# Projections by token halves, norms inside the stage, attention on row halves: a two-block transformer kernel in fp32

## The chip, the cores and the metric

One core of one Trainium2 chip. The metric is the device time of the kernel in microseconds, median of three runs.

## What is computed

Three residual layers on x of 1024 tokens by 1024 channels, then a last norm. All of it is fp32.

```python
# layer 0 (even): attention and Fourier mixing; ctx: 256 context tokens
h = modulate(x, norm_g[0], shift, scale)                  # rms norm
proj = h @ w_in                                           # Fourier, q, k, v, gate
s = einsum('bqhmd,bkhmd->bhmqk', q, k) * DH ** -0.5       # 4 heads, 2 maps m, DH = 64, 1280 keys
p = softmax(s); a = p[:, :, 0] - lam * p[:, :, 1]         # difference of the two maps
o = einsum('bhqk,bkhv->bqhv', a, v)
ao = rms_norm(o, subln_g) * (1 - lam_init)
x = x + gate * ((concat([fourier_mix(u), ao]) * silu(g)) @ w_out)
# layer 1 (odd): x + gate * ((bg * conv3(cg * xt) * silu(g)) @ w_out)
# layer 2: h = rms_norm(x); y = sigmoid(m_a) * y_rglru + sigmoid(m_b) * y_hgrn2; x = x + y @ w_out
#          x = x + square(relu(rms_norm(x) @ w_up)) @ w_down
return rms_norm(x, norm_final)
```

## The kernel before

**Layout.** Channels lie on partitions, tokens along the free axis: X is [128, 8, 1024], eight tiles of 128 channels. A product of fp32 precision is made of three fp32r products: the weights are split in a high part Whi (ScalarE copies Wraw, L420) and a low part Wlo (POOL subtracts, L383), the operand in Hh and Hl. A **unit** is 128 columns of a weight matrix: per half of 512 tokens and per channel tile k a triple Whi x Hh, Whi x Hl, Wlo x Hh of 512 columns (`products`, L1282 to L1284, and `half`, L1392 to L1394), 48 products in all, into one of two accumulators `acc(0)`, `acc(1)` of two PSUM banks. Weights, too, have two slots: SyncE loads a slot (512 KB) when POOL has split the unit before last in it, ScalarE splits when TensorE has finished the unit that used Whi of this slot. Semaphores count units (`lo_ready`, `acc_ready`, `acc_free`). Stages follow each other in the list PHASES: four, q, k, v, g (even input), eo (even output projection, 8 units), oi (odd input, 32), oo (8), rg, hg (input of layer 2, 32 and 40), ho (8), mlp (64: four times 8 up and 8 down).

**Projections.** `dense` (PE) runs eight units for eo, oo and ho. For each unit VectorE adds the result to its tile of X (L829, L831), ScalarE squares the tile (L445), and TensorE sums the squares over partitions by a product with a matrix of ones in plain fp32 (`norm_sum`, L1296; one fp32 product of 512 columns shows as two half products in the trace). The sum of unit k is put behind unit k + 1. After the last one ScalarE takes the root (L434), VectorE the reciprocal of 1024 columns (L803), and then tile by tile a scaling (L809), the high part on ScalarE (L439) and the low part on VectorE (L814) in Hh and Hl; the next stage's first unit waits for each tile (`h_tile`). Before each projection all engines meet (`rendezvous`), and y (the input of the projection) is split into Hh and Hl (`split_y`, L449, L820): Y has to be whole, as Hh and Hl are the operand of the stage that makes it.

**Attention.** 32 blocks of 128 queries: all eight token blocks of head 0, then head 1, and so on, in a loop of two blocks. POOL copies the queries into a zeroed tile (L403), so that for map m only its 64 rows are filled. For each map: three fp32 products of 128 rows give 1280 scores in 2.5 PSUM banks (L1538), VectorE takes the maximum (L1028), ScalarE the exp with its sum (L601). VectorE combines both maps (L1035 to L1039). The ten transposes of the weights (L1552), their copies (L607), the ten products with v (L1559) and the scaled copy of the output (L612) run one block behind. `tile_pair` writes this order out for PE and ACT. After the loop the norm of the outputs, their transposes and the product with the gate follow on their own (L1052 to L1066), and x is loaded again (L635), since attention uses its place.

**End.** The last norm ("n4") writes X; TensorE transposes X back to token rows (L1754), ScalarE copies each of 8 row blocks (L794), SyncE stores it (L375).

Queues: SyncE issues all weight loads in the order of the units and the stores; ScalarE's queue loads tables, masks and x.

## Time and profile before

| | us |
|---|---|
| runs (3) | 3238.88, 3241.10, 3241.49 |
| median | 3241.1 |
| profiled execution, its own time | 3242.23 |
| its span | 3240.4 |
| TensorE busy (14314 products) | 3026.3 |
| VectorE, ScalarE, POOL busy | 1234.8, 918.5, 538.8 |
| mean granted TensorE clock | 0.965 of full |

The profile shows one execution. PE is TensorE's products, PEld its weight loads, DVE VectorE, ACT ScalarE, POOL GpSimd, SP SyncE. A busy time is the union of the instructions' times. Products overlap in the pipeline, so the spacing of their starts tells their cost, not their length. PEclk is the granted TensorE clock as a share of 2.4 GHz; 0.5 is 1.2 GHz.

### The profile page before, as it was taken

To read this page: it belongs to the slowest core of one execution; us is meant where nothing else is said; L and a number is where in the kernel's file an instruction comes from. 1 tells how busy PE (TensorE), PEld (TensorE's weight loads), DVE (VectorE), ACT (ScalarE), POOL (GpSimd) and SP (SyncE) were. 2 spreads that over 40 slices of the span, in tenths; PEclk is the share of its full clock that TensorE was granted. 3 is DMA by queue.
4 is the path that set the end of the run, shared out by engine and by line. 5 is a ranking of instruction groups with operands and counts; after the bars stand their busy time and mean duration, and the time that the engine had idled before them with its cause. 6 is when DMAs were issued, how large, how long until landed. Compare 5 with 4: busy or idle time off the path is not lost.

```text
span 3240.4 us, 36419 instructions
## 1 busy us (share of the span) xinstructions
PE 3026.3 (93%) x14314; PEld 2427.0 (75%) x14314; DVE 1234.8 (38%) x1284; ACT 918.5 (28%) x1027; POOL 538.8 (17%) x285
## 2 busy tenths in 40 slices
PE   6999989996889999889998999999897999999996
PEld 4878766664668887667777888888775888888874
DVE  4476126664232222244444566565524212121112
ACT  4332225552122122144442222222222202121221
POOL 0111100001112222112221111111011222222220
PEclk8999999997989999989999999999898999999998
DMA  6111520001111111111111111111010111111111
GB/s 200 65 33 39 176 78 0 0 7 72 32 39 45 52 45 46 33 39 45 45 45 42 33 40 33 33 36 37 20 39 26 46 52 45 52 45 47 50 46 52
DMA packets 249035, 155.11 MB, mean 48 GB/s; under 512 B 5360, under 2 KB 245360, under 8 KB 248432
## 3 DMA queue, kind: packets, MB, share of 16 engines
q1 hardware_dynamic: 247360, 146.10, 15.2%
q10 hardware_dynamic: 1584, 7.70, 0.6%
q8 instruction: 69, 1.13, 0.1%
q14 instruction: 22, 0.18, 0.0%
HBM read 149.59 MB, written 4.19 MB: 47 GB/s over the span
## 4 chain that ended last, share of the span: by engine, by line
PE 51%; issue 39%; POOL 4%; DVE 3%; ACT 1%; DVEq 0%; DMA 0%; POOLq 0%; ACTq 0%
PE PS L1282 8%; PE PS L1284 8%; PE PS L1283 8%; PE PS L1392 5%; PE PS L1394 5%; PE PS L1393 5%; POOL Wlo L383 4%; PE PS L1538 4%; PE PS L1650 3%; PE PS L1559 2%; PE PS L1552 1%; PE PS L1296 1%; PE PS L1655 1%; PE PS L1684 0%; PE PS L1638 0%
## 5 line engine op out<-in xcount | busy, mean ns | idle before, releaser
L383 POOL TENSOR_TENSOR Wlo<-Wraw,Whi 128x1024 fp32r<-128x1024 f32 (+1 forms) x216 | 519.4, 2405 | 2366.4 <-ACT Whi L420 2365.9
L1282 PE MATMUL PS<-Hh,Whi 128*128 128x512 f32 x1792 | 720.4, 402 | 78.5 <-DVE Hl L814 56.3
L1283 PE MATMUL PS<-Hl,Whi 128*128 128x512 f32 x1792 | 706.7, 394 | 0.0
L1284 PE MATMUL PS<-Hh,Wlo 128*128 128x512 f32 x1792 | 706.3, 394 | 0.0
L1282 PEld LDWEIGHTS PS<-Hh,Whi 128*128 128x128 f32 x1792 | 341.1, 190 | 175.6 <-issue 68.6
L1392 PE MATMUL PS<-Hh,Whi 128*128 128x512 f32 x992 | 400.4, 404 | 14.2 <-ACTq L277 8.9
L1283 PEld LDWEIGHTS PS<-Hl,Whi 128*128 128x128 f32 x1792 | 342.5, 191 | 73.2 <-issue 4.3
L1284 PEld LDWEIGHTS PS<-Hh,Wlo 128*128 128x128 f32 x1792 | 342.1, 191 | 72.7
L1394 PE MATMUL PS<-Hh,Wlo 128*128 128x512 f32 x992 | 388.1, 391 | 0.0
L1393 PE MATMUL PS<-Hl,Whi 128*128 128x512 f32 x992 | 387.7, 391 | 0.0
L420 ACT ACTIVATE Whi<-Wraw 128x1024 fp32r<-128x1024 f32 (+1 forms) x216 | 223.8, 1037 | 373.3 <-PE PS L1284 350.5
L1392 PEld LDWEIGHTS PS<-Hh,Whi 128*128 128x128 f32 x992 | 187.3, 189 | 58.3 <-issue 13.5
L1394 PEld LDWEIGHTS PS<-Hh,Wlo 128*128 128x128 f32 x992 | 186.9, 188 | 40.5
L1393 PEld LDWEIGHTS PS<-Hl,Whi 128*128 128x128 f32 x992 | 187.4, 189 | 36.7 <-issue 1.0
L1282 PE MATMUL PS<-Uh,Whi 128*128 128x512 f32 x512 | 202.2, 395 | 0.6 <-DVE Ul L1258 0.3
L1284 PE MATMUL PS<-Uh,Wlo 128*128 128x512 f32 x512 | 199.3, 389 | 0.0
L1283 PE MATMUL PS<-Ul,Whi 128*128 128x512 f32 x512 | 199.2, 389 | 0.0
L1261 DVE TENSOR_TENSOR X<-X,PS 128x1024 f32<-128x1024 f32 x32 | 39.1, 1221 | 307.1 <-PE PS L1284 307.1
L1538 PE MATMUL PS<-kT,qs 128*128 (+1 forms) x384 | 150.0, 527 | 5.3 <-POOL qs L403 2.7
L1255 DVE TENSOR_TENSOR sq<-ut 128x1024 f32<-128x1024 f32 x32 | 39.2, 1225 | 246.0 <-ACT ut L777 246.0
L445 ACT ACTIVATE sq<-X 128x1024 f32 (+1 forms) x32 | 33.9, 1060 | 329.5 <-PE PS L1296 145.4
L1538 PEld LDWEIGHTS PS<-kT,qs 128*128 128x128 f32 x384 | 68.9, 193 | 68.1 <-issue 68.1
(286 smaller groups left out, 3419.9 us busy)
## 6 DMA issues: line engine op xcount, KB each, us to landing
Wraw<-in_w_in SPq DMA_DIRECT2D x64, 512.0 KB, 4.0
adaV<-in_ada_w SPq DMA_DIRECT2D x16, 1024.0 KB, 5.2
Wraw<-in_odd_w_in SPq DMA_DIRECT2D x32, 512.0 KB, 4.0
Wraw<-in_w_up SPq DMA_DIRECT2D x32, 512.0 KB, 4.0
Wraw<-in_w_down SPq DMA_DIRECT2D x32, 512.0 KB, 3.9
Wraw<-in_even_w_in SPq DMA_DIRECT2D x24, 512.0 KB, 3.8
adaW<-in_ada_w SPq DMA_DIRECT2D x8, 1024.0 KB, 8.8
X<-in_x SPq DMA_DIRECT2D x8, 512.0 KB, 8.0
```

Source lines behind the costliest of these rows:

```text
L383: pool.tensor_tensor(Wlo[:, slot, 0:tiles, :], Wraw[:, slot, 0:tiles, :], Whi[:, slot, 0:tiles, :].bitcast(F32), ALU.subtract).then_inc(lo ...
L420: act.activation(Whi[:, slot, 0:tiles, :], Wraw[:, slot, 0:tiles, :], COPY).then_inc(hi_ready, 1)
L1255: tt(sq2[:, k % 2, :], ut[:, k % 2, :], ut[:, k % 2, :], ALU.mult).then_inc(sem("usq_ready"), 1)
L1282: mm(out, Whi[:, slot, k, :], hi[:, k, c], start=(k == 0), stop=False)
L1283: mm(out, Whi[:, slot, k, :], lo[:, k, c], start=False, stop=False)
L1284: last = mm(out, Wlo[:, slot, k, :], hi[:, k, c], start=False, stop=(k == kt - 1))
L1392: mm(out, Whi[:, slot, k, :], Hh[:, k, c], start=(k == 0), stop=False)
L1393: mm(out, Whi[:, slot, k, :], Hl[:, k, c], start=False, stop=False)
L1394: last = mm(out, Wlo[:, slot, k, :], Hh[:, k, c], start=False, stop=(k == KT - 1))
L1538: ins = mm(PS[:, 1536 * m + c:1536 * m + c + w].rearrange("p (a n) -> p a n", a=1), qs[:, s, m, :], kT[:, bass.ds(h, 1), c:c + w], start=T ...
L1559: ins = mm(bank(7, P), probT[:, s, t, :], vT[:, t, bass.ds(hc, P)], start=(t == 0), stop=(t == 9))
L1650: ins = mm(bank(4 + lev % 2, 64, c * 64).rearrange("p (b l) -> p b l", l=L), z, right, start=True, stop=True)
```

## The change

1. **Projections by token halves.** eo, oo, ho and the last down projection have 14 units in place of 8: tiles 0 and 1 over all tokens, then tiles 2 to 7 for tokens 0 to 511, then the same for tokens 512 to 1023. The weights of tiles 2 to 7 are loaded and split twice. After unit 7 the first half of X is complete.
2. **Norms within the stage.** VectorE adds the squares of a half in `sacc`, TensorE sums once per half. Root, reciprocal, scaling and splitting of the first half lie in units 8 to 12, those of the second half in the opening of the next stage, whose first two units run their first halves first. ScalarE now splits the weights of unit n + 2 before it squares tile n.
3. **Two operand regions in turn.** Stages read Hh, Hl or Bh, Bl (in the place of Y and of the scratch tiles), so y is split while it is made (oi: each tile; ho: in the last head) and the meetings of all engines before and after the projections go. The first eo and ho units run in quarters (four or two channel tiles) between the last operations of attention and of the last head.
4. **Attention.** Order by token block with the four heads inside; the two maps' queries lie in rows 0 to 63 and 64 to 127 of one tile, and each map is a product on its 64 rows. SCALE goes into the queries. The transposed weights have 2.5 banks of their own and one copy, outputs are squared on POOL and summed on VectorE per block, and the norm and transposes of the outputs run per token half.
5. **Output by channel.** X is stored as it lies, [128, 8 x 1024], in 8 stores, each when its two half tiles are scaled; the reordering to tokens is on the host. The 64 transposes and 8 copies go.
6. Loops over units are written out. The loads of x after attention are SyncE's.

```diff
-PHASES = [("four", 4), ("q", 4), ("k", 4), ("v", 4), ("g", 8), ("eo", 8), ("oi", 32), ("oo", 8),
-          ("rg", 32), ("hg", 40), ("ho", 8), ("mlp", 64)]
+PHASES = [("four", 4), ("q", 4), ("k", 4), ("v", 4), ("g", 8), ("eo", 14), ("oi", 32), ("oo", 14),
+          ("rg", 32), ("hg", 40), ("ho", 14), ("mlp", 70)]
...
+    Bh = at("Bh", y0, [KT, N], F32R)
+    Bl = at("Bl", t0, [KT, N], F32R)
...
+        def projection(i, base, shift):
+
+            def square(n):
+                evacuated(act, 0, 2, base + n)
+                act.wait_ge(sem("sq_added"), 13 * i + (0 if n < 2 else max(n - 2, 1)))
...
+            for n in range(14):
+                split_next(0, 2, base + n + 1)
+                square(n)
+                if n == 7:
+                    root(0)
+                if 9 <= n < 13 and i < 3:
+                    high(0, 2 * (n - 9))
+                    high(0, 2 * (n - 9) + 1)
+            root(1)
+            if i < 3:
+                for k in range(KT):
+                    high(1, k)
...
+            for n in range(14):
+                if n == 8:
+                    invert(0)
+                residual(n)
+                if n:
+                    add_square(n)
+                if 9 <= n < 13:
+                    for k in (2 * (n - 9), 2 * (n - 9) + 1):
+                        scaled(0, k)
+                    for k in (2 * (n - 9), 2 * (n - 9) + 1):
+                        if i < 3:
+                            low(0, k)
+            invert(1)
+            scaled(1, 0)
             for k in range(KT):
+                if k + 1 < KT:
+                    scaled(1, k + 1)
+                if i < 3:
+                    low(1, k)
...
+        def square_sum(i, h):
+
+            pe.wait_ge(sem("sq_added"), 13 * i + 6 * h + 7)
+            mm(bank(4 + h), ones, sacc[:, h, :], start=True, stop=True).then_inc(sem("ss_psum"), 1)
+
+        def by_halves(i, base, rhs):
+
+            for n in range(2, 14):
+                u, h = base + n, 0 if n < 8 else 1
+                claim(u)
+                c = slice(h * 512, h * 512 + 512)
+                for k in range(KT):
+                    last = triple(u, k, acc(u % 2)[:, 0:512], rhs, c)
+                    if n == 8 and k == 3:
+                        square_sum(i, 0)
+                last.then_inc(acc_ready, 1)
+
+        def opening(i, u, rhs):
+
+            pe.wait_ge(sem("norm_lo"), 16 * i + 8)
+            half(u, 0, rhs, lambda: square_sum(i, 1))
+            half(u + 1, 0, rhs)
+            c = slice(512, 1024)
+            for k in range(KT):
+                pe.wait_ge(sem("norm_lo"), 16 * i + 9 + k)
+                last = triple(u, k, acc(u % 2)[:, c], rhs, c)
+                if k % 2:
+                    triple(u + 1, k // 2, acc((u + 1) % 2)[:, c], rhs, c)
...
+        def scores(b):
+
+            s, h = b % 2, b % HEADS
+            pe.wait_ge(sem("qs_ready"), b + 1)
+            if b:
+                pe.wait_ge(sem("exp_ready"), 2 * b)
+            for i, (k1, w1, k0, w0) in enumerate(((0, 256, 0, 512), (256, 512, 512, 512), (768, 512, 1024, 256))):
+                mm(PS[:, S1 + k1:S1 + k1 + w1], qs[64:128, s, :], kT[64:128, h, k1:k1 + w1], start=True, stop=True).then_inc(sem("s1_psum"), 1)
+                if i == 2:
+                    pe.wait_ge(sem("s1_psum"), 3 * b + 1)
+                mm(PS[:, S0 + k0:S0 + k0 + w0], qs[0:64, s, :], kT[0:64, h, k0:k0 + w0], start=True, stop=True).then_inc(sem("s0_psum"), 1)
...
+        for c in range(BLOCKS):
+            scores(c)
+            if c >= 2:
+                turn(c - 2)
+            if c >= 3:
+                output(c - 3)
...
+        for c in range(BLOCKS):
+            if c >= 4:
+                output_out(c - 4)
+            if c >= 3:
+                weights_out(c - 3)
+            exps(c)
...
+        for c in range(BLOCKS + 1):
+            if c < BLOCKS:
+                shifts(c)
+            if c >= 1:
+                combine(c - 1)
+            if c >= 6:
+                block_sum(c - 6)
...
+        level(last, 4)
+        quad(o0, (0, 1), (Bh, Bl), odd_wait)
+        level(last, 5)
+        quad(o0, (2, 3), (Bh, Bl), odd_wait)
+        level(last, 6)
+        keys_turn(last)
+        quad(o0 + 1, (0, 1), (Bh, Bl), odd_wait)
+        increments(last)
+        quad(o0 + 1, (2, 3), (Bh, Bl), odd_wait)
+        output_rows(last)
+        quad(o0, (4, 5), (Bh, Bl), odd_wait)
+        output_turn(last)
+        quad(o0, (6, 7), (Bh, Bl), odd_wait)
+        quad(o0 + 1, (4, 5, 6, 7), (Bh, Bl), odd_wait)
+        by_halves(2, o0, (Bh, Bl))
...
-    out = nc.dram_tensor("out", (1, N, D), F32, kind="ExternalOutput").ap()
+    out = nc.dram_tensor("out", (P, KT * N), F32, kind="ExternalOutput").ap()
```

In `quad` a quarter of a unit is run for the channel tiles `ks` and the given halves; `claim` waits for the unit's weights and accumulator; `triple` is the three products above.

## Rows read from the trace of the kernel before

**Rows 1.** The profile page, part 1 and costliest groups (busy, mean ns | idle before, releaser).

```profile
PE 3026.3 (93%) x14314; PEld 2427.0 (75%) x14314; DVE 1234.8 (38%) x1284; ACT 918.5 (28%) x1027; POOL 538.8 (17%) x285
...
L383 POOL TENSOR_TENSOR Wlo<-Wraw,Whi 128x1024 fp32r<-128x1024 f32 (+1 forms) x216 | 519.4, 2405 | 2366.4 <-ACT Whi L420 2365.9
...
L420 ACT ACTIVATE Whi<-Wraw 128x1024 fp32r<-128x1024 f32 (+1 forms) x216 | 223.8, 1037 | 373.3 <-PE PS L1284 350.5
```

**Rows 2.** Busy time of each engine by stretch; columns as in its first line.

```profile
core 0: us, PE busy (x) PEld busy (x) DVE busy (x) ACT busy (x) POOL busy (x), PEclk, DMA share, GB/s
484.00:730.00 246.00, 228.84 (x1195) 154.96 (x1196) 147.33 (x198) 131.53 (x225) 17.70 (x54) 1.00 0.01 2
876.00:912.00 36.00, 16.21 (x33) 8.07 (x32) 29.30 (x19) 13.69 (x12) 0.65 (x1) 0.61 0.00 0
912.00:1256.00 344.00, 344.00 (x1513) 284.52 (x1511) 69.71 (x47) 66.76 (x62) 76.65 (x32) 1.00 0.17 49
1256.00:1260.00 4.00, 0.17 (x1) 0.00 (x0) 2.44 (x3) 2.39 (x3) 0.00 (x0) 0.93 0.00 0
1708.00:1718.00 10.00, 1.10 (x4) 0.65 (x3) 7.10 (x5) 3.73 (x4) 0.00 (x0) 0.77 0.10 22
2322.00:2358.00 36.00, 19.14 (x98) 17.47 (x97) 19.32 (x28) 7.03 (x8) 0.00 (x0) 0.68 0.00 1
```

**Rows 3.** Timeline of POOL and VectorE in oi (start, us, engine, operation [idle before, releaser]).

```profile
930.94 2.39 POOL L383 TENSOR_TENSOR Wlo<-Wraw,Whi 128x1024 fp32r<-128x1024 f32 x1 [7.50 <-ACT Whi L420]
...
931.28 2.60 DVE L1084 TENSOR_SCALAR cv<-up,P 128x1024 f32<-128x1024 f32 x1 [0.25 <-issue]
...
974.46 2.39 POOL L383 TENSOR_TENSOR Wlo<-Wraw,Whi 128x1024 fp32r<-128x1024 f32 x1 [7.50 <-ACT Whi L420]
```

**Rows 4.** Timeline of one attention block.

```profile
573.31 2.31 PE L1538 MATMUL PS<-kT,qs 128*128 x6
...
573.98 1.55 DVE L1039 SCALAR_TENSOR_TENSOR prob<-prob,acol 128x1280 f32<-128x1280 f32 x1
...
575.66 1.49 DVE L1028 TENSOR_REDUCE acol<-PS 128x1 f32<-128x1280 f32 x1
...
575.67 1.09 PE L1552 MATMUL PS<-basic,prob 128*128 128x128 f32 x8
...
577.42 1.33 ACT L601 ACTIVATE prob<-PS,acol 128x1280 f32<-128x1280 f32 x1
...
579.74 2.49 PE L1559 MATMUL PS<-vT,probT 128*128 x20 [0.61 <-ACT probT L607]
```

**Rows 5.** Timeline of TensorE at attention's first and last products, and eo's first.

```profile
450.05 2.90 PE L1538 MATMUL PS<-kT,qs 128*128 128x512 f32 x3 [2.66 <-POOL qs L403]
...
724.75 2.31 PE L1538 MATMUL PS<-kT,qs 128*128 x6
...
734.96 4.63 PE L1559 MATMUL PS<-vT,probT 128*128 128x128 f32 x20 [0.47 <-ACT probT L607]
...
774.78 0.77 PE L1282 MATMUL PS<-Hh,Whi 128*128 128x512 f32 x1 [3.80 <-DVE Hl L820]
```

**Rows 6.** Timeline of eo: sums of squares, the reciprocal, the next stage's first product.

```profile
799.77 1.88 PE L1296 MATMUL PS<-sq,basic 128*128 128x512 f32 x4
...
875.65 1.88 PE L1296 MATMUL PS<-sq,basic 128*128 128x512 f32 x4
...
881.84 6.55 DVE L803 RECIPROCAL Rn<-Rn 128x1024 f32<-128x1024 f32 x1 [4.48 <-ACT Rn L434]
...
892.72 0.76 PE L1282 MATMUL PS<-Hh,Whi 128*128 128x512 f32 x1 [12.07 <-DVE Hl L814]
```

**Rows 7.** Groups of TensorE instructions by line.

```profile
L1296 PE MATMUL PS<-sq,basic 128*128 128x512 f32 x128 | 60.5, 595 | 4.0 <-ACT sq L445 4.0
```

**Rows 8.** DMA issues of the page (KB each, median us to landing).

```profile
Wraw<-in_w_in SPq DMA_DIRECT2D x64, 512.0 KB, 4.0
```

**Rows 9.** Timeline of the end: last sums of squares and the scaling.

```profile
3197.89 1.88 PE L1296 MATMUL PS<-sq,basic 128*128 128x512 f32 x4
...
3210.30 10.92 DVE L809 SCALAR_TENSOR_TENSOR X<-X,P,Rn 128x1024 f32<-128x1024 f32 x8
```

More of the change, by code:

```diff
@@ L1261, in dve_program, with claim @@
                 tt(X[:, k, :], X[:, k, :], acc(k % 2), ALU.add).then_inc(acc_free[k % 2], 1)
             dve.drain()
-        dve.drain()
-        norm("n4", X, N, None, None, lambda k: P2[:, COL2["norm_final_2"] + k:COL2["norm_final_2"] + k + 1], None)
+        projection(3, DOWN, plain, lambda k: P2[:, COL2["norm_final_2"] + k:COL2["norm_final_2"] + k + 1], None)
     def pe_program(pe):
         mm = pe.matmul
-        def products(i, n, b, rhs, start=0, kt=KT, first=False):
+        def claim(u):
+            pe.wait_ge(lo_ready, u + 3)
+            pe.wait_ge(acc_free[u % 2], u // 2 + 1)
@@ new lines, in triple, with half, whole @@
+            return mm(out, Wlo[:, u % 2, k, :], hi[:, k, c], start=False, stop=(k == KT - 1))
+        def half(u, h, rhs=(Hh, Hl), mid=None):
+            if h == 0:
+                claim(u)
+            c = slice(h * 512, h * 512 + 512)
+            for k in range(KT):
+                last = triple(u, k, acc(u % 2)[:, c], rhs, c)
+                if k == 3 and mid:
+                    mid()
+            return last
+        def whole(u, rhs):
+            half(u, 0, rhs)
+            half(u, 1, rhs).then_inc(acc_ready, 1)
@@ L1558, in output @@
             for t in range(10):
[L1559 removed]
+                ins = mm(PS[:, OUT:OUT + P], probT[:, b % 2, t, :], vT[:, t, h * P:(h + 1) * P], start=(t == 0), stop=(t == 9))
             ins.then_inc(sem("o_psum"), 1)
[L1562 to L1569 removed]
@@ new lines, in pe_program @@
+        turn(31)
+        output(30)
+        output_turn_half(0)
+        output(31)
+        quad(e0, A, (Hh, Hl), even_wait, (1,))
+        quad(e0 + 1, A, (Hh, Hl), even_wait, (0,))
+        output_turn_half(1)
+        quad(e0 + 1, A, (Hh, Hl), even_wait, (1,))
+        quad(e0, B, (Hh, Hl), even_wait)
+        quad(e0 + 1, B, (Hh, Hl), even_wait)
+        by_halves(0, e0, (Hh, Hl))
+        opening(0, BASE["oi"], (Bh, Bl))
+        for u in range(BASE["oi"] + 2, BASE["oo"]):
+            whole(u, (Bh, Bl))
@@ L1615, in pe_program @@
[L1615 removed]
+                claim(u)
                 if j == 4:
```

864 lines of the change are left out of this document (419 added, 445 removed).

## The prediction

> **What bounds the kernel now.** I read the page's totals first: TensorE is busy for 93% of the span [rows 1]. That average hides two kinds of stretch, so the table by stretch comes next. Inside a stage of plain products (912 to 1256) TensorE works for 344.00 of 344 us at full clock [rows 2]. Nothing there can be won. The time lies where it stops or does work that isn't a product of the model: the norm behind each projection (876 to 912: 16.21 us busy of 36), the hand-overs (1256 to 1260, 1708 to 1718, 2322 to 2358), the end, and attention, where it is 93% busy at full clock but with operands half full of zeros [rows 2]. The timelines of these places give the prices. About 0.2% (6.5 us) is what a measurement of this kernel can tell from no change.
>
> One unit of weights is 48 products of 512 columns. Four units of the odd input stage lie 974.46 - 930.94 = 43.52 us apart [rows 3], so a unit is 10.88 us and a half unit 5.44.
>
> **Attention loop.** Now a block of 128 queries pays two score sets of 2.31 us, ten transposes (8 in 1.09) and 20 half products in 2.49 [rows 4]: about 8.6 us. From the first score (450.05) to the end of the last (724.75 + 2.31) it is 277.0 us for 32 blocks [rows 4, 5].
> Afterwards the two maps sit on rows 0-63 and 64-127 of the array. If they run side by side, both sets take about what one takes, plus a lead-in: 2.4 us. TensorE's sum is then 2.4 + 1.3 + 2.5 = 6.2 us. The softmax loop is as long: scores 2.4; maximum of the last mixed bank 0.69 (estimate: 1280 elements take 1.49 [rows 4], so 0.16 + 1.04 ns each); a small maximum with its drain 0.3; exp 1.33; the second exp waits for a 1024-element maximum (1.22 by the same estimate) and starts at 5.2; it ends at 6.55, and the next scores wait for both. VectorE's sum (1.49 x 2, a second fixed part for each extra maximum, the combination 1.55 and its scalars) is about 6.3. Three engines within 0.4 us of each other don't mesh perfectly; I take 6.8 us a block. No row shows half-row products, so the bounds are 6.5 (side by side) and 8.5 (one after the other: 4.6 us of scores in the same loop). I take the side near 6.5, since two operands in disjoint rows share nothing the rows name. The zero fill and one copy go, so it starts 1 us earlier: last scores end at 449 + 31 x 6.8 + 2.4 = 662.2 against 727.1. **-64.9**.
>
> The Trainium skill ("TensorE: Matmul & The Clock Gate", Part 3) measured 3.07x for four row tiles, not 4x. Two tiles at that efficiency would take 3.0 us instead of 2.4 and the total would be about 3010. The same skill ("TensorEngine Tiling", Key Properties) says that a change of tiling mode drains the engine; each block changes twice. No row here shows either.
>
> **Attention's end.** Now from the last score to the first projection product (774.78) is 47.7 us, partly at half clock: the last output takes 4.63 us instead of 2.49 [rows 4, 5]. With 1.4 us lost to the slow first products this is 49.1. Afterwards squares and sums are made per block on POOL and VectorE, and four quarter units (10.9 us of projection) fill waits. Following ScalarE in order: two exps, table load and root, then copy, output, copy for blocks 28 to 31, the last output lands about 24 us after the last score; scale, turn, split of the second half some 10 us later. That is 34 us, less the 10.9 us of work done in it, plus 3 for a clock that won't stay up: 26. **-23**.
>
> **Three projections with their norm.** From 776.2 to the effective start of the next stage (its end 1256.2 less 32 units = 908.0) there are 131.8 us for 87.0 us of products: 44.8 us lost. It is: eight sums of squares, each 4 half products (units and sums alternate six times from 799.77 to 875.65, 75.88 / 6 = 12.65 us against 10.88, so 1.77 each, 14.1 [rows 6]; all 128 half products of the four norms: [rows 7]); and behind the last unit a root, a reciprocal of 6.55 us for 1024 columns, and the first split, until 892.72 [rows 6], then products that wait for every tile's low part (16.21 of 36 us busy [rows 2]). Two more projections have this pattern, and I take the same loss for them.
> Afterwards VectorE adds the squares and TensorE sums once per half (0.9 us). I walk one projection from the end of unit 7 (t = 0). ScalarE splits the next weights first (1.04 [rows 1]), squares (0.6), POOL makes the low part (2.39). Here POOL matters: a VectorE operation on SBUF alone that meets POOL's subtraction ends only with it (931.28 + 2.60, POOL until 933.33; [rows 3]). So the adding of squares waits until 3.6 and ends at 4.3; TensorE wanted the sum at 2.7: 1.6 lost, 0.9 for the sum. Root and half reciprocal (3.3, half of 6.55) end at 9.4. In units 9 to 12 VectorE owes each time a residual, an add, two scalings, two low parts (0.7 to 0.75 each, half of 1.28 plus the fixed part) and must sit out about 1.7 us of POOL: some 6.5 us against 5.44. The lag reaches 4.7 us at the end of unit 13, where the next stage opens: 4.7 lost. There the second sum is waited for 0.55 and costs 0.9; root, reciprocal 3.3, then 1.6 us a tile end at 61.3, when TensorE still has six triples: 2.1 lost. Sum with small ones: 11. Bounds: 4.4 (no lag) and 20 (every one of twelve half units 0.75 late). 3 x (44.8 - 11) = **-101.4**.
>
> **Weights.** 24 more loads of 512 KB, 4.0 us to land [rows 8]. A slot's round is 4.0 + 1.04 + 2.39 = 7.5 us in the 10.9 us of two half units; the part after a unit's end is 3.6 to 5.1 of 5.44. Hidden; if POOL also waits for VectorE the cover is 0.3 us.
>
> **Hand-overs.** 1256 to 1260: 4 us and a slow start, split as made: **-4.8**. 1708 to 1718: 8.9 us of waiting for all engines, now only ScalarE waits, and TensorE has a unit whose weights are ready: **-8.9**. 2322 to 2358: 19.14 busy of 36, much of it at half clock [rows 2]. Quarter units fill it, but VectorE gets 7 low parts (1.2 each, by the estimate above) and ScalarE 7 copies on the way; the last split comes some 3 us later than now. I count **-11** (bounds -4, -18).
>
> **Last projection and end.** Sums of squares before the last unit's end 7 x 1.77 = 12.4, afterwards 2.5: **-9.9**. From 3197.9 to 3240.4 is 42.5: sum, root, 6.55, eight scalings 10.92 [rows 9], 64 transposes, copies, stores. Afterwards: residual, square, add 2.2; sum and root 1.7; 3.3; eight half scalings 6; last store 2.7: 16.2. **-26.3**. The first half's stores lie under the second half.
>
> Sum: -64.9 - 23 - 101.4 - 4.8 - 8.9 - 11 - 9.9 - 26.3 = -250. The profiled execution took 3242.2 us (span 3240.4), 1.1 above the median shown. 3242.2 - 250.2 = 2992.0, against the median **2991**.
>
> **Rivals.**
> (a) The row halves do not overlap: that part then doesn't do what it is built for. 8.5 us a block: +1.7 x 32 = 54, so 3045. For it: no row shows overlap, and each score product already runs as two halves. Chance 0.2.
> (b) The weights come late in the half units, because POOL waits for VectorE as well: 1 us on each of 48 is +48, 3039. For it: the cover of 0.3 us. Against: POOL's 216 subtractions average 2405 ns now. Chance 0.08.
> (c) The lag behind POOL does not build up: 11 becomes 4.4, so 2971. Chance 0.05.
> (d) Slower than before: half-row products leave TensorE at 1.2 GHz throughout attention and also don't overlap. Place: the loop. Price: 8.6 us x 4.63 / 2.49 = 16.0 a block, +9.2 x 32 = 294, so 3285. It decides from 6.8 + 250 / 32 = 14.6 us a block. Against it: full clock in all of 484 to 730 with 0.6 us of waits a block [rows 2]. Chance 0.02.
> The forecast keeps 0.65, itself good to about 35 us: 0.3 us a block is 10, each of the norms 9, the two ends 8 each.
> Range 2945 to 3055: it takes in (a), (b), (c). Faster 0.97, same 0.01, slower 0.02: only (d) and what I haven't seen reach 3235.
>
> **What would show it.** Period of the scores: 6.8, or 8.5. Half-row products whose times overlap. Spacing of the half units 5.44 for n = 2 to 8. The wait before the opening of each stage about 4.7 us, on the low part. 31 to 35 us from last score to the start of the quarters 4 to 7. VectorE's adding of squares waiting for POOL. End 16 us after the last product. The prediction is wrong if the block period is over 7.3 with overlap, or if the half units are paced by POOL.

## The result, and the profile after

The kernel after takes 3001.8 us (median; the profiled execution 3001.18, span 2999.1), the kernel before 3241.3. The ratio is 0.9259, 95% interval 0.9246 to 0.9273: 239.5 us less, where 250 were forecast (2991 us, range 2945 to 3055). One of the four executions of the kernel after took 4168.2 us at a granted clock of 0.651 (and one of four of the kernel with all mends, below, 3626.1 us at 0.749); ratios and intervals are of the executions at the usual clock. Both profiled executions against each other give 3242.2 - 3001.2 = 241.0, and the working below goes by these two.

The page of the kernel after: part 1, and of part 5 some groups, beside [rows 1] (busy us, mean ns | idle before, releaser).

```profile
PE 2866.4 (96%) x14138; PEld 2356.7 (79%) x14138; DVE 1370.8 (46%) x1509; ACT 904.8 (30%) x1013; POOL 615.0 (21%) x316
...
L398 POOL TENSOR_TENSOR Wlo<-Wraw,Whi 128x1024 fp32r<-128x1024 f32 (+1 forms) x240 | 572.6, 2386 | 2163.2 <-ACT Whi L453 2163.2
...
L861 DVE TENSOR_TENSOR sacc<-sacc,sqs 128x512 f32<-128x512 f32 x48 | 98.7, 2056 | 40.9 <-ACT sqs L472 40.9
L1669 PE MATMUL PS<-kT,qs 64*128 64x512 f32 (+1 forms) x192 | 84.0, 575 | 32.2 <-ACT prob L644 27.5
```

TensorE's share rose from 93 to 96%, and it has fewer half products. The line to stop at is L861: VectorE's new adding of squares, 512 columns, takes 2056 ns, where its neighbours of the same size take about 750. That was forecast; what it costs was not forecast fully.

**The ledger by stage.** A landmark is a product that can be named in both kernels. A stage's effective start is the end of a later landmark less the products up to it (10.886 us a unit). The gain of each piece, in us:

```
piece                                         forecast   measured
attention, last scores' end 727.1 -> 663.7      64.9       63.4
attention's end, 49.1 -> 26.4                   23         22.7
three projections with norm, 134.4 -> 45.2     101.4       89
hand-over to oo, 5.4 -> 0.8                      4.8        4.6
waits inside rg, 8.3 -> 0                        0          8.3
hand-over to hg, 8.9 -> 0                        8.9        8.9
last diagonal of hg to ho, 68.9 -> 60.3         11          8.6
last projection's sums                           9.9       10.1
from the last product to the end, 42.5 -> 16.2  26.3       26.3
sum                                            250.2      241.9
```

(The 0.9 by which the sum exceeds 241.0 is what the landmarks are good for.) By the table seven of nine terms are right within 2.5 us. The three projections are 12 us short, and the waits inside rg, which I had not counted, gave 8.3 back: before, TensorE waited 1.60 and 0.47 us for GpSimd's low parts in each of rg's four groups, afterwards nowhere there.

No run was made on why, but the traces show where it went. ScalarE behind the fifth unit of a group, in the kernel before and then in the one after:

```profile
1521.94 1.28 ACT L680 ACT_TABLE_LOAD   x1 [3.98 <-PE PS L1626]
1523.24 1.12 ACT L680 ACTIVATE ra<-PS,P 128x1024 f32<-128x1024 f32 x1
```

```profile
1368.07 1.28 ACT L726 ACT_TABLE_LOAD   x1
1371.95 1.12 ACT L726 ACTIVATE ra<-PS,P 128x1024 f32<-128x1024 f32 x1 [2.60 <-PE PS L1761]
```

Before, the table load of 1.28 us stands behind the wait for TensorE, and the next weights' split behind it; afterwards it is done while ScalarE waits. That is most of the 1.60. For the 0.47, VectorE's three steps of the convolution lay 0.18 us apart before (L1111 at 1485.40, 1486.86, 1488.32) and follow each other without a pause afterwards (L1207, 4.01 us for all three from 1335.75), so the split behind them comes 0.5 us earlier. The order of the operations is the same in both; what changed there is item 6, the loops written out. That this is the cause was not tested.

Three readings of the table are coarse. It takes a sum of squares at 0.54 us, where one costs TensorE 0.9 to 1.1 (experiment 8). It takes rg's loss up to the third unit's first product, ahead of some 1.8 us that the half clock costs behind that wait (next part). And the hand-over to hg gave 12 us, not 8.9: from the last product of rg to the last head's products of hk and hq in hg (1708.2 to 2287.93 before, 1552.7 to 2120.36 after) the distance shrank by 12 us, since TensorE in the kernel before ran at half clock behind its wait, too:

```profile
1717.47 0.80 PE L1392 MATMUL PS<-Hh,Whi 128*128 128x512 f32 x1 [8.90 <-ACTq L277]
```

```profile
1717.50:1723.60 6.10, 6.10 (x14) 4.76 (x15) 0.91 (x1) 2.34 (x2) 2.37 (x1) 0.50 0.16 41
```

Counted product by product, the three projections lose some 13, 21 and 15 us afterwards, 49 in all instead of 45.

**Where the projections lose.** TensorE in the kernel after, first products behind a wait (start, us, engine, operation [idle before <-releaser]): the first sum in eo, the opening of oi, the third unit of rg.

```profile
748.06 1.13 PE L1426 MATMUL PS<-sacc,basic 128*128 128x512 f32 x2 [1.50 <-DVE sacc L861]
...
783.54 0.79 PE L1384 MATMUL PS<-Bh,Whi 128*128 128x512 f32 x1 [4.26 <-DVE Bl L879]
784.13 0.63 PE L1385 MATMUL PS<-Bl,Whi 128*128 128x512 f32 x1
...
1266.04 0.79 PE L1384 MATMUL PS<-Bh,Whi 128*128 128x512 f32 x1 [7.54 <-POOL Wlo L398]
```

The wait for the first sum is 1.50 us (forecast 1.6), that ahead of the opening 4.25 (forecast 4.7). Both stand in all three projections. The third line I had no term for: 7.54 us in rg, 1.11 in oi, 3.51 in mlp. And the second holds something else: the next product starts 0.59 us later and those after it 0.43 us apart, where the usual step is 0.227. TensorE runs at half clock. The table by stretch of the same kernel shows it (us, busy time by engine, then PEclk, the granted clock as a share of 2.4 GHz):

```profile
748.06:752.00 3.94, 3.94 (x16) 2.94 (x17) 2.06 (x1) 0.69 (x1) 0.00 (x0) 1.00 0.46 135
779.30:783.50 4.20, 0.00 (x0) 0.00 (x0) 3.88 (x5) 2.33 (x3) 0.41 (x1) 0.76 0.45 125
783.50:788.20 4.70, 4.66 (x11) 3.69 (x12) 2.20 (x2) 0.63 (x1) 2.38 (x1) 0.50 0.13 31
788.20:792.00 3.80, 3.80 (x16) 2.74 (x16) 1.62 (x1) 0.69 (x1) 0.00 (x0) 0.99 0.36 106
...
1266.00:1270.60 4.60, 4.56 (x13) 3.62 (x14) 4.02 (x4) 0.00 (x0) 0.00 (x0) 0.61 0.23 59
...
2159.80:2164.00 4.20, 4.20 (x10) 3.29 (x11) 3.94 (x6) 0.10 (x1) 0.00 (x0) 0.51 0.00 0
...
2193.20:2197.00 3.80, 3.80 (x9) 3.03 (x10) 0.00 (x0) 0.00 (x0) 0.00 (x0) 0.50 0.02 4
...
2305.40:2309.00 3.60, 3.59 (x16) 2.98 (x17) 2.26 (x2) 2.01 (x2) 0.44 (x1) 1.00 0.52 146
```

After the wait of 1.50 us the clock is 1.00, and after that of 3.51 (2301.90 to 2305.41) too, though not in every run (last section). After 4.25 us it is 0.50 for 4.7 us: 11 products where 21 fit, a further 2.3 us. The same pattern stands behind the other two openings (1232.37, 2275.59) and behind the waits of 7.54, 5.01 and 4.36 us (1266.04, 2159.80, 2193.18). So each of these waits costs 1.5 to 2.4 us more than its length, in busy time that no list of gaps shows. The Trainium skill ("TensorE: Matmul & The Clock Gate", HAM oscillation — how this bites in real kernels) describes this pattern, a wait for data after which the work starts at half rate; the trace agrees, and I had priced it for attention's end only.

**Why the third unit waits.** ScalarE in the kernel after, at the opening of rg, and GpSimd behind it:

```profile
1255.49 1.02 ACT L715 ACTIVATE xp<-PS 128x1024 f32<-128x1024 f32 x1 [2.21 <-DVEq L1197]
1261.48 1.06 ACT L717 ACTIVATE xch<-xc 128x1024 fp32r<-128x1024 f32 x1 [4.96 <-DVE xc L1207]
1262.44 1.04 ACT L453 ACTIVATE Whi<-Wraw 128x1024 fp32r<-128x1024 f32 x1
...
1263.56 2.43 POOL L398 TENSOR_TENSOR Wlo<-Wraw,Whi 128x1024 fp32r<-128x1024 f32 x1 [28.82 <-ACT Whi L453]
```

The split of the third unit's weights (L453) stands in ScalarE's program behind the convolution's high part (L717), which waits 4.96 us for VectorE. Unit 0, whose slot the split needs, had ended at 1255.6, some 7 us ahead of it.

**Attention.** A block has the period 6.51 us in the steady part (scores at 498.66 and 505.17), and TensorE waits 0.61 us in it. The chain of one block, VectorE, ScalarE, then TensorE's next scores:

```profile
501.29 0.68 DVE L1100 TENSOR_REDUCE acol<-PS 128x2 f32<-128x512 f32 x1
...
502.24 1.33 ACT L644 ACTIVATE prob<-PS,acol 128x1280 f32<-128x1280 f32 x1 [2.34 <-DVE acol L1102]
...
503.60 1.33 ACT L644 ACTIVATE prob<-PS,acol 128x1280 f32<-128x1280 f32 x1
...
505.17 0.45 PE L1669 MATMUL PS<-kT,qs 64*128 64x256 f32 x1 [0.61 <-ACT prob L644]
505.17 0.69 PE L1672 MATMUL PS<-kT,qs 64*128 64x512 f32 x1
```

2.63 us from the scores' start to the last mixed maximum, 0.95 to the first exponential, 1.36 to the second, 1.57 to the next scores. The two last lines, one of rows 64 to 127 and one of rows 0 to 63, start together: the halves do run side by side. The start was worse than forecast: first scores at 452.19 instead of 449, and the first four cycles take 8.61, 8.10, 8.59 and 8.15 us; TensorE's clock is 0.50 in 447.5 to 456.8 there.

### The profile page after: what moved, and what is told of

The parts are those of the page before. It is cut to its first block, busy times and chain, and to the rows that moved or that the text cites. A ratio compares the mean times of both kernels' runs of the same rounds, so it can differ in the third digit from the quotient of the medians.

```text
span 2999.1 us, 34350 instructions
## 1 busy us (share of the span) xinstructions
PE 2866.4 (96%) x14138; PEld 2356.7 (79%) x14138; DVE 1370.8 (46%) x1509; ACT 904.8 (30%) x1013; POOL 615.0 (21%) x316
## 3 DMA queue, kind: packets, MB, share of 16 engines
q10 hardware_dynamic: 1440, 3.51, 0.3%
## 4 chain that ended last, share of the span: by engine, by line
issue 61%; PE 25%; POOL 8%; ACT 3%; DVE 1%; DVEq 1%; POOLq 0%; ACTq 0%
POOL Wlo L398 8%; PE PS L1384 8%; PE PS L1386 7%; PE PS L1385 7%; ACT prob L644 3%; PE PS L1669 2%; DVEq L1101 1%; DVE acol L1097 0%; PE PS L1672 0%; POOLq L402 0%; DVE acol L1102 0%; DVE X L872 0%; PE PS L1690 0%; DVE Rn L866 0%; POOLq L397 0%
## 5 line engine op out<-in xcount | busy, mean ns | idle before, releaser
L1384 PE MATMUL PS<-Bh,Whi 128*128 128x512 f32 x2176 | 862.9, 397 | 28.6 <-DVE Bl L879 9.6
L1386 PE MATMUL PS<-Bh,Wlo 128*128 128x512 f32 x2176 | 850.9, 391 | 0.0
L1385 PE MATMUL PS<-Bl,Whi 128*128 128x512 f32 x2176 | 850.7, 391 | 0.0
L1384 PEld LDWEIGHTS PS<-Bh,Whi 128*128 128x128 f32 x2176 | 411.1, 189 | 120.4 <-DVE Bl L879 14.3
L1386 PEld LDWEIGHTS PS<-Bh,Wlo 128*128 128x128 f32 x2176 | 410.7, 189 | 86.9
L1385 PEld LDWEIGHTS PS<-Bl,Whi 128*128 128x128 f32 x2176 | 411.4, 189 | 83.4 <-issue 1.0
L1384 PE MATMUL PS<-Hh,Whi 128*128 128x512 f32 x1120 | 444.7, 397 | 13.8 <-POOL Wlo L398 5.8
L1385 PE MATMUL PS<-Hl,Whi 128*128 128x512 f32 x1120 | 436.9, 390 | 0.0
L1386 PE MATMUL PS<-Hh,Wlo 128*128 128x512 f32 x1120 | 436.8, 390 | 0.0
L453 ACT ACTIVATE Whi<-Wraw 128x1024 fp32r<-128x1024 f32 (+1 forms) x240 | 249.5, 1040 | 552.6 <-PE PS L1386 534.2
L1385 PEld LDWEIGHTS PS<-Hl,Whi 128*128 128x128 f32 x1120 | 210.8, 188 | 43.9 <-issue 1.7
L861 DVE TENSOR_TENSOR sacc<-sacc,sqs 128x512 f32<-128x512 f32 x48 | 98.7, 2056 | 40.9 <-ACT sqs L472 40.9
```

Of the source, the lines that this page charges most:

```text
L453: act.activation(Whi[:, slot, 0:tiles, :], Wraw[:, slot, 0:tiles, :], COPY).then_inc(hi_ready, 1)
L861: tt(sacc[:, h, :], sacc[:, h, :], sqs[:, n % 2, :], ALU.add).then_inc(sem("sq_added"), 1)
L1384: mm(out, Whi[:, u % 2, k, :], hi[:, k, c], start=(k == 0), stop=False)
L1385: mm(out, Whi[:, u % 2, k, :], lo[:, k, c], start=False, stop=False)
L1386: return mm(out, Wlo[:, u % 2, k, :], hi[:, k, c], start=False, stop=(k == KT - 1))
```

## The experiments

Twelve kernels were run. Each is the kernel after with one edit, unless said otherwise.

**1. The row halves one behind the other.**

```diff
-for i, (k1, w1, k0, w0) in enumerate(...):   # S1 and S0 products in turn
+for k0, w0 in ((0, 512), (512, 512), (1024, 256)):     # all of S0
+for k1, w1 in ((256, 512), (768, 512), (0, 256)):      # then all of S1
+    if k1 == 0: pe.wait_ge(sem("s0_psum"), 3 * b + 3)  # its last product alone waits for the S0 list
```

> The kernel after, with only the order of the six score products of a block changed: the three of rows 0 to 63 first, then the three of rows 64 to 127, so that products of the two row halves no longer stand beside each other except where the first list meets the second. Theory (the two row halves work at the same time, and that is why a block takes 6.51 us): the scores of a block take about 4.3 us instead of 2.4, TensorE's work per block rises from 5.9 to about 7.8 us and becomes the bound, period 7.8 to 8.5 us, the whole 3042 to 3065 us. Rival (the halves hardly overlap, the period is set by the softmax chain of VectorE and ScalarE alone): period and time stay, 6.5 us and 2998 to 3004 us.

Measured: 3039.2 us (one run), period 7.34 us. The period rose by 0.83 us only, since products of rows 64 to 127 still began 0.94 us after the first of rows 0 to 63, before those had ended. Between theory and rival; the order alone doesn't part the halves. So it was done again with a wait between the lists:

```diff
+pe.wait_ge(sem("s0_psum"), 3 * b + 3)                  # before the S1 products
```

> The kernel after, with the score products of a block in the order of the first run (rows 0 to 63, then rows 64 to 127) and a wait between the two lists, so that no product of one half can run beside one of the other; in the first run they still ran side by side for about 1 us a block, and the period went to 7.34 us only. Theory (the overlap is what halves the scores, and the block's period is one chain, scores, maxima, two exponentials, next scores): scores take 4.3 to 4.5 us instead of 2.35, the chain and so the period 8.5 to 8.7 us, the whole 3065 to 3076 us. Rival (the period has other slack, as the first run's smaller loss could mean): 7.3 to 8.0 us, 3038 to 3055 us.

Measured: 3122.2 us (one run), 120 more than the kernel after, well over both expectations. Where the clock is full, the scores take 4.8 us and the period is 8.87 (564.27 to 573.14), near the theory. But the clock is not always full. Stretches of this run (PE busy first, granted clock third from the end):

```profile
705.60:719.10 13.50, 12.86 (x66) 8.42 (x65) 8.49 (x14) 6.38 (x10) 1.79 (x4) 1.00 0.01 2
719.30:725.80 6.50, 6.50 (x20) 4.28 (x19) 2.51 (x7) 1.85 (x3) 0.00 (x0) 0.50 0.00 0
726.10:739.50 13.40, 12.77 (x65) 8.36 (x65) 8.39 (x14) 6.29 (x10) 1.79 (x4) 1.00 0.00 1
...
740.00:750.00 10.00, 10.00 (x39) 6.76 (x38) 4.82 (x9) 4.27 (x6) 0.89 (x2) 0.68 0.00 0
750.00:760.00 10.00, 9.37 (x46) 5.92 (x45) 6.38 (x12) 4.17 (x6) 0.89 (x2) 1.00 0.00 0
```

TensorE is busy for 94 to 100% of the time and has no wait over 0.52 us, and still its clock falls to the lower level, 0.50, for some 6.8 us in every two blocks, which then take 20.45 us (8.88 and 11.57) instead of 17.7. The edit is that the two halves of the rows work one behind the other, with a wait between them; in the kernel after (484 to 660) and in the run before this one (500 to 690, period 7.34) the clock is 1.00. So what goes with the fall is shown, but which part of the edit makes it, the half rows or the wait, was not told apart. The 120 us lie in the loop: from the last score to the end it takes 2337.7 us, in the kernel after 2335.4. Some 75 of them are the period of 8.87 instead of 6.51 at full clock, the rest is the clock. My rival (d) had such a fall of the clock and was priced for one that is low throughout.

**2. The third unit's split early.** In the first group of oi, rg and mlp, for rg:

```diff
 got(act, 0, 2, b + m)
+if i == 0 and m == 0:
+    split_next(0, 2, b + 1)
 act.activation(xp[:, 3:3 + N], acc(m), COPY)
```

> The kernel after, with only ScalarE's order changed at three places: in the first group of each stage behind a projection it makes the high part of the third unit's weights ahead of reading the first accumulator, instead of behind it (and, in the recurrent stage, behind the convolution's high part). Theory (the third unit waits for its weights because its split stands behind ScalarE work that itself waits for VectorE): the waits of 1.10, 7.53 and 3.51 us ahead of the third unit fall to at most 1 us each, the whole 2989 to 2992 us. Rival (the split is late because the first unit of the stage ends late, so the place in the order is worth little; or the wait moves to the fourth unit): under 3 us gained, 2998 to 3002 us.

Measured: 2996.9 us. All three waits fell to 0.29 us, as the theory has it. But in rg the fourth unit then waited 5.48 us for its low part, whose split stood behind the next high part, and the clock was 0.50 behind that wait: the rival's second half was right too. Of the 11.3 us of waiting, 4.9 were kept by the medians, 4.1 in the profiled executions, and of these 1.2 lie in attention, which the edit doesn't touch (last score's end 662.53 instead of 663.76). So it was 3 to 5 us, between theory and rival.

**3. The squares in PSUM.**

```diff
-act.activation(sqs[:, n % 2, :], X[...], SQUARE)
+act.activation(bank(6 + n % 2), X[...], SQUARE)
-tt(sacc[:, h, :], sacc[:, h, :], sqs[:, n % 2, :], ALU.add)
+tt(sacc[:, h, :], sacc[:, h, :], bank(6 + n % 2), ALU.add)
```

> The kernel after, with only the tile of the squares moved from SBUF to two free PSUM banks: ScalarE writes them there and VectorE adds them from there; instructions, order and waits are the same. Theory (the adding of squares takes 2056 ns instead of about 700 because VectorE and GpSimd hold each other up where both operands lie in SBUF, and this sets both the wait for the first sum and the lag ahead of the stages' openings): the add takes about 0.7 us, the waits of 1.50 us fall to at most 0.3, those of 4.25 us to at most 1, the 2.16 us ahead of the last sum to about 1, the whole 2981 to 2988 us. Rival A (the add is long for another reason, such as its start being counted while it waits for its semaphore): duration and waits stay, 3001 us. Rival B (the add gets short, but the lag ahead of the openings comes from the pause of 0.70 us in which VectorE waits for ScalarE's square): only the sums' waits go, 2994 to 2997 us.

Measured: 2978.5 us, ratio to before 0.9190 (0.9175 to 0.9205). GpSimd and VectorE in the kernel after, and then in this one (the first line of each is GpSimd's):

```profile
758.60 2.40 POOL L398 TENSOR_TENSOR Wlo<-Wraw,Whi 128x1024 fp32r<-128x1024 f32 x1 [3.04 <-ACT Whi L453]
...
759.07 2.48 DVE L861 TENSOR_TENSOR sacc<-sacc,sqs 128x512 f32<-128x512 f32 x1 [0.92 <-ACT sqs L472]
761.64 1.41 DVE L874 SCALAR_TENSOR_TENSOR tn<-X,Dv,Rn 128x512 f32<-128x512 f32 x2
```

```profile
756.62 2.40 POOL L398 TENSOR_TENSOR Wlo<-Wraw,Whi 128x1024 fp32r<-128x1024 f32 x1 [3.04 <-ACT Whi L453]
...
757.07 0.69 DVE L861 TENSOR_TENSOR sacc<-sacc,PS 128x512 f32<-128x512 f32 x1 [0.89 <-ACT PS L472]
757.85 2.39 DVE L874 SCALAR_TENSOR_TENSOR tn<-X,Dv,Rn 128x512 f32<-128x512 f32 x2
```

The add met GpSimd's subtraction in both. With both inputs in SBUF it ended 0.55 us behind it, with one in PSUM it ran through in 0.69 us, and the next operation, whose inputs are both in SBUF, waited instead (2.39 us for a pair that takes 1.41). A rival is that an input from PSUM is faster of itself. The kernel after answers that: 46 of its 48 adds meet a subtraction, and each of them ends 0.55 us behind it, while the two that meet none, behind the last weights, take 0.69 us with both inputs in SBUF:

```profile
2979.02 0.69 DVE L861 TENSOR_TENSOR sacc<-sacc,sqs 128x512 f32<-128x512 f32 x1 [0.70 <-ACT sqs L472]
```

The Trainium skill ("SBUF — State Buffer", Who interferes with whom) says just this: a VectorE instruction with two SBUF inputs contends with a GpSimd instruction that reads SBUF, one with at most one doesn't. The first sum's wait is gone, the opening's is 1.19 us instead of 4.25, and the clock behind it is 1.00. The theory's sum was 13 to 20 us, so the run is faster than it said. Of the 23 measured, 1.5 + 3.1 + some 2 of clock in each of three projections and 1.5 in the last account for 21. The last sum's wait stayed (2.13 us): nothing of GpSimd's lies there, it is residual, square and add in a row.

**4. The queries first.**

```diff
-splits(0, BASE["eo"] + 2)
+splits(0, BASE["eo"]); split(BASE["eo"], 0)
 ...
+if b == 1: split(BASE["eo"] + 1, 1)        # behind the queries of blocks 0 and 1
```

> The kernel after, with only GpSimd's order changed where attention begins: the queries of blocks 0 and 1 are scaled ahead of the low part of the second weight unit of the output projection, instead of behind it. Theory (the pause of 4.7 us ahead of the first scores is GpSimd's, and TensorE's granted clock, 0.50 of full in 447.5 to 456.8 and again in 460.8 to 463.5 and 468.9 to 472, is low because of that pause): first scores at about 448.7 instead of 452.2, the first blocks' scores take 2.4 us instead of 4.0 to 4.6, and attention is through 8 to 12 us earlier, the whole 2989 to 2993 us. Rival (the clock falls anyway, since the first blocks leave TensorE pauses of 4 us each while only scores are in the pipeline): the start comes 3.5 us earlier and no more, 2997 to 2998 us.

Measured: 2996.6 us. First scores at 448.60, 3.6 us earlier, and the sixth block's, in the steady part, at 488.58 instead of 492.15, again 3.6: the rival's mechanism. The clock was 0.53 in 449 to 454 all the same. Then the pauses were filled:

```diff
+filler(8)                                   # 128x128 products, unread
 scores(c)
+filler(24 if c < 2 else 0)
```

> The kernel of the run before this one with the queries first, and with products that nobody reads added on TensorE: 8 of 128 columns ahead of the first scores and 24 behind the scores of blocks 0 and 1, into a PSUM region that is unused then. Theory (the granted clock of 0.50 to 0.53 in 447.5 to 454 comes from TensorE's own pauses, and falls away when they are filled): the scores of blocks 1 to 3 take 2.4 us instead of about 4, and the time is 3 to 6 us shorter than the 2996.6 of the queries first, 2990.5 to 2993.5 us. Rival (the clock is low there whatever TensorE does, or the added products delay the scores by as much as the clock gives back): 2996 to 3001 us.

Measured: 2999.3 us. The clock rose, as the theory has it (0.96 to 1.00 in 452 to 468; in the last two of these stretches the run before had 0.58 and 0.76):

```profile
449.00:452.00 3.00, 3.00 (x11) 2.10 (x12) 0.00 (x0) 0.00 (x0) 0.91 (x1) 0.50 0.00 0
452.00:454.00 2.00, 2.00 (x13) 1.17 (x10) 1.54 (x3) 0.00 (x0) 0.29 (x1) 0.96 0.00 0
454.00:460.00 6.00, 6.00 (x52) 5.59 (x51) 1.89 (x4) 2.79 (x4) 1.23 (x2) 1.00 0.01 3
...
472.70:479.40 6.70, 5.95 (x19) 3.68 (x20) 3.69 (x6) 2.01 (x4) 0.53 (x1) 0.50 0.01 2
```

But the sixth block's scores began at 488.69, no earlier. The 24 added products take 5.62 us each time, longer than the pauses of 3.97 and 4.09 us that they fill, and behind the last of them the clock fell once more, so that the fourth cycle took 8.73 us. The rival's second half was right.

**5. The norm behind the stage.** ScalarE's and VectorE's first-half tiles moved behind the last half unit:

```diff
-    if 9 <= n < 13 and i < 3:
-        high(0, 2 * (n - 9)); high(0, 2 * (n - 9) + 1)
+for k in range(KT if i < 3 else 0):         # behind the loop over n; VectorE alike
+    high(0, k)
```

> The kernel after, with the norm of the first token half no longer made within the projection: in the first three projections ScalarE and VectorE scale and split the first half's tiles behind the last half unit. Everything else stays (two regions, half units, sums on VectorE). Theory (what the second region buys is that the eight first-half tiles, four pairs of 3.0 us on VectorE, lie beside TensorE's products, and what is left of a projection's loss is VectorE's chain behind its last half unit): the wait ahead of a stage's opening grows from 4.25 to 15 or 16 us, the last low part of the second half comes about 35 us behind the end of the last half unit instead of 26.8, so each of the three projections loses about 8 us more and the whole is 3022 to 3030 us. Rival A (the loss is the opening's wait alone): 11 us more each, 3033 to 3037 us. Rival B (the chain of the second half sets the time in any case): 3001 to 3008 us.

Measured: 3043.3 us (one run), 41.5 more. The opening's wait is 17.09 us instead of 4.25, and the clock behind it is 0.50. From the opening to the end of its two units it takes 27.44 us, against 26.91 in the kernel after: that distance did not shrink, although the second half's chain could have begun earlier, because TensorE makes the second sum behind the opening's first products. So the whole wait comes on top, and rival A's mechanism is the right one, though the time lies above its figure as well (3033 to 3037): the wait grew by 12.8 us, not 11. Making half of the norm within the stage is worth 13.8 us a projection, 12.8 of them this wait.

**6. The end alone.** The kernel before, with X stored by channel as it is scaled and nothing turned:

```diff
+for k in range(KT):
+    sp.wait_ge(sem("scaled"), KT * NORM["n4"] + k + 1)
+    sp.dma_start(ok[:, k, :], X[:, k, :]).then_inc(sem("stored0"), 16)
```

> The kernel before, with only its end changed: the scaled tiles of X are stored by channel as they are made, and the transposes, the copies out of PSUM and the token-major stores are left out (the reordering to tokens lies outside the kernel, as in the kernel after). Theory (the end's gain has two parts, the turning of the output and the halving of reciprocal and scaling): the last tile is scaled at the same place, 23.3 us behind the last sum, and its store lands 2.6 to 4 us later, so the time is 15 to 17 us shorter, 3224 to 3226 us, and the other 10 us of the 26.3 belong to the token halves. Rival (eight stores of 512 KB queue behind one another and the last lands late): 8 to 12 us shorter, 3229 to 3233 us.

Measured: 3223.1 us (one run), beside 3242.3 for the kernel before. VectorE at the end of this run:

```profile
3195.09 1.22 DVE L1254 TENSOR_TENSOR X<-X,PS 128x1024 f32<-128x1024 f32 x1 [11.43 <-PE PS L1277]
3200.62 6.55 DVE L796 RECIPROCAL Rn<-Rn 128x1024 f32<-128x1024 f32 x1 [4.31 <-ACT Rn L433]
3207.30 10.92 DVE L802 SCALAR_TENSOR_TENSOR X<-X,P,Rn 128x1024 f32<-128x1024 f32 x8
```

The scaling ends at 3218.22, the span at 3221.3: 3.1 us for the last store. From the last residual it is 26.2 us instead of 42.3, so 16.1 of the 26.3 belong to the order of the output, and the other 10.2 to the token halves. The theory holds for the end; the time is 0.9 below its range, since 3 us of the whole lie ahead of 3195, in parts that are the same in both.

**7. All mends.** Experiments 2 (with the fourth split of rg early as well), 3 and 4 together, and VectorE scaling its pair ahead of the add:

```diff
 residual(n)
+if 9 <= n < 13: scaled(0, 2 * (n - 9)); scaled(0, 2 * (n - 9) + 1)
 if n: add_square(n)
-if 9 <= n < 13: scaled(...)
```

> The kernel after, with the squares in PSUM, the queries first, the third unit's split early in the three openings and the fourth one's too in the recurrent stage, and VectorE scaling its pair of first-half tiles ahead of adding the square, so that ScalarE's squaring lies beside it. Theory (the losses are different places of the chain and add up): 22.9 us of the squares, 4.8 of the queries, 0.8 + 7.2 + 3.2 of the splits and 1.2 ahead of each of three openings come off 3001.4, 2956 to 2962 us; no wait over 1 us ahead of any stage's first four units. Rival (the waits move on to later units or to the low parts of the second half, as the 5.48 us ahead of the fourth unit did): 2963 to 2974 us.

Measured: 2964.7 to 2972.0 us, ratio 0.9161 (0.9143 to 0.9180). That is the rival's figure, but not its mechanism: all waits for weights in the openings were at most 0.30 us, and what remained was the opening's own wait, 2.38 us, more than without the reordering. GpSimd and VectorE in this run:

```profile
747.90 3.55 DVE L887 SCALAR_TENSOR_TENSOR tn<-X,Dv,Rn 128x512 f32<-128x512 f32 x2
751.38 0.67 DVE L874 TENSOR_TENSOR sacc<-sacc,PS 128x512 f32<-128x512 f32 x1
...
748.43 2.47 POOL L398 TENSOR_TENSOR Wlo<-Wraw,Whi 128x1024 fp32r<-128x1024 f32 x1 [3.04 <-ACT Whi L456]
```

The pair now stands where GpSimd subtracts and takes 3.55 us; it, too, ends 0.55 us behind the subtraction. With the old order back:

> The kernel of all mends, with VectorE's old order back (the square is added ahead of scaling the pair). Theory (with the new order the scaling stood beside GpSimd's split and took 2.7 to 3.5 us a pair instead of 1.4, in place of the adding that it had held up before): scaling is back at 1.4 to 2.4 us a pair, the wait ahead of the openings at 1.2 us instead of 2.38, the whole 2960 to 2963.5 us. Rival (the 4 us that all mends fell short lie in the attention part or in the splits' new places): 2964 to 2968 us.

Measured: 2959.9 us (2959.5 to 2962.4), ratio 0.9135 (0.9123 to 0.9148). The opening's wait is 1.19 us again. This is the fastest kernel of the study, 42 us under the kernel after. One more edit on top of it:

```diff
 def opening(i, u, rhs):
+    square_sum(i, 1)
     pe.wait_ge(sem("norm_lo"), 16 * i + 8)
-    half(u, 0, rhs, lambda: square_sum(i, 1))
+    half(u, 0, rhs)
```

> The kernel of the run before, with TensorE summing the second half's squares ahead of a stage's first product, not behind its first twelve. Theory (root, reciprocal, scaling and splitting of the second half all hang on this sum, and the sum hangs on the opening, so every us of the opening's wait comes back in the second half's low parts): the opening starts about 1.4 us later, the last low part comes about 1.8 us earlier, each of three stages gains 1 to 2 us, the whole 2956 to 2960 us. Rival (TensorE, held at the sum for the last square, loses as much as the chain gains): within 1 us of the run before.

Measured: 2967.4 us, 7.5 slower. TensorE waited 3.39 us for the sum instead of 1.19 for the low part, since VectorE's add stands behind the last pair of low parts, and the clock was 0.62 in 777.0 to 781.5. The second half's waits did go (no wait over 0.2 us in it), so its chain was shortened, but from the last half unit to the third unit's start it takes 28.2 us instead of 26.3. Worse than the rival. Of the 7.5 us some 2.4 lie in attention, which the edit doesn't touch (last score's end 660.02 instead of 657.65).

**8. The sums on TensorE again.**

```diff
-if n: add_square(n)                         # VectorE
+mm(bank(4 + h), ones, sqs[:, n % 2, :], start=False, stop=(n in (7, 13)))   # TensorE, each n; its waits left out here
```

> The kernel after, with one part undone: TensorE again sums the squares of each tile (16 products of 512 columns a projection instead of 2), and VectorE adds none. Theory (the moved sums save TensorE 14 products of 0.54 us in each of four projections, 30 us, but the adding, slowed beside GpSimd's split, gives 5 to 8 us back in each of them): the waits of 1.50 us fall to under 0.3 and those of 4.25 to under 0.5 us, the second halves' low parts come earlier, and the whole is within 2995 to 3008 us, about what it was. Rival (the adding on VectorE costs nothing of note, so the sums' full 30 us come back): 3026 to 3033 us.

Measured: 3027.0 us, ratio 0.9341. The rival's figure, but not its mechanism. The waits of 1.50 and 4.25 us are gone, as the theory has it; my price of a sum was wrong. In the last projection, which has no norm to hide, TensorE's way from mlp's third unit to its last product is 690.3 us instead of 677.5. Of these 12.8 us, 1.7 are the clock at its start, 0.50 in 2319.0 to 2322.3, where the kernel after has 1.00; and the wait of 1.5 has gone from the way. That leaves 12.6 us for 14 more sums, 0.9 each, not the 0.54 that I took from a mean over half products ([rows 6] gave 0.89). So the four projections pay some 50 us gross and get 25 back. Moving the sums to VectorE is worth 25 us, and would be worth 48 with the squares in PSUM.

## Why the prediction was right, and where it was wrong

The forecast case came true: the whole is 10 us off, inside its range, and none of the rivals held.

- **Attention loop, -64.9: right (-63.4).** Its two halves erred against each other. The period is 6.51 us, not 6.8: the three engines do mesh, since the loop is one chain. The start cost some 9 us more than counted: GpSimd's split stands ahead of the first queries (experiment 4), and the first four cycles run partly at half clock. Rival (a), no overlap, is excluded by the pairs of products that start together and by experiment 1. The efficiency that the Trainium skill measured for four row tiles doesn't carry over to two: the scores take 2.35 us (498.66 to 501.01), not the 3.0 that I estimated from it ("TensorE: Matmul & The Clock Gate", Part 3), and the transposes start at 501.01, with no gap for the change of tiling.
- **Attention's end, -23: right (26.4 us against 26).** No run tests its parts. One sign came late: the quarters over tiles 4 to 7 start at 700.16, 36 us behind the last score, not 31 to 35, with other products right ahead of them.
- **Three projections, -101.4: short by 12 in the ledger, by 16 counted product by product.** This is the step that failed, the sum of 11 us a projection, though the whole came out right. Its walk was right for the first sum (1.50 against 1.6) and the opening's wait (4.25 against 4.7), and experiment 3 shows the reason given for both, GpSimd's subtraction, to be the right one. It stopped too early: the "Weights" paragraph found the splits hidden within a projection, and nothing followed ScalarE on into the next stage, where the third unit waits 1.10, 7.53 and 3.51 us behind work of that stage (experiments 2 and 7). And it had no price for the clock, 1.5 to 2.4 us behind each opening's wait and 1.8 behind rg's third unit. What the sum did count, two sums, two waits and the second half's tail, cost 9.5 us where I had 10.8; the third unit and the clock made 13, 21 and 15 us of it (12.6, 18.2 and 14.4 in the ledger's coarser reading), not 11.
- **Waits inside rg, not in the sum: +8.3.** They stood in the trace of before as gaps of 1.60 and 0.47 us four times and I passed over them. They and the 3 us that the hand-over to hg gave beyond its wait cancel most of what the projections fell short, which is luck.
- **Hand-overs: right for oo; hg 12 instead of 8.9; ho 8.6 instead of 11.** For hg I took the wait alone and not the half clock behind it, which went with it. Ahead of ho TensorE still waits 5.01, 1.51 and 4.36 us, and pays for the clock twice.
- **Last projection and end: right (10.1 and 26.3).** Experiment 6 confirms the split of the end, 16.1 for the order of the output and 10.2 for the halves.
- **Rival (b), half units paced by GpSimd: excluded.** Within the projections no wait over 0.3 us but for the first sum. **Rival (c), no lag:** it is what experiment 3 makes of this kernel, 2978.5, where I had 2971.

## What to carry to other kernels

Walk every engine's program order past the end of the part you change: a split that needs nothing but a free slot can still stand behind work that waits for a third engine. Where VectorE and GpSimd share a stretch, see which operands lie in SBUF; moving one of two inputs to PSUM took 23 us off here, while changing the order only chose another victim. Price a wait on TensorE by what comes behind it too: those of 4.25 us and more cost another 1.5 to 2.4 here at half clock, and one that goes gives that back as well.

## What the runs showed that I had not expected

- TensorE's clock was 0.50 for some 6.8 us in every two blocks, with TensorE busy for all but 0 to 6% of the time and no wait over 0.52 us, when the score products used one half of the rows at a time (experiment 1, second run). With both halves at work side by side it stayed at 1.00.
- Products of the other row half slip past: with three products of one half issued ahead of three of the other, the second list began 0.94 us behind the start of the first.
- The clock behind a wait is not given by the wait's length. Behind the wait of 3.51 us ahead of mlp's third unit it is 1.00 in the kernel after and 0.50 in the runs of experiments 5 (2345.1 to 2349.0) and 8 (2319.0 to 2322.3). In the run of all mends two waits of 2.38 us are followed by 1.00 (771.4 to 775.4) and 0.57 (1213.4 to 1217.4). Behind every wait of 4.24 us and more it was 0.50 to 0.63 over the next 4 us. So one place can differ by 1.7 us between two runs without the edit having touched it.
